# Expert weights in one 16 KB piece per partition, and transposes that read columns with a step

## The chip, the cores and the metric

The kernel runs on one core of one Trainium2 chip. The metric is device time in microseconds (us), from one launch of the whole kernel; lower is better. TensorE's granted clock has two levels, 2.4 GHz (shown as 1.00) and 1.2 GHz (0.50).

## The reference

One layer of a hybrid decoder on 4096 tokens of width 1024, in float32. The first half (norm, one combined projection, sliding-window attention beside a short gated convolution, output projection) gives `h`. The second half is a mixture of experts: each token goes to the best 1 of 4 groups and there to the best 2 of 8 experts, so there are 8192 assignments over 32 experts.

```python
order = jnp.argsort(eid)                       # assignments sorted by expert
xbuf = zeros.at[dest].set(xt[tok_s])           # blocks of 128 rows, one expert each
def expert_block(args):
    xb, e = args                               # xb: 128 x 1024
    return (jax.nn.silu(xb @ w_g[e]) * (xb @ w_u[e])) @ w_d[e]
y = ybuf[dest] * gate_s[:, None]               # w_g, w_u: 1024 x 512; w_d: 512 x 1024
return jax.ops.segment_sum(y, tok_s, num_segments=n_tok)
```

A sum over the 1024 (or 512) rows of a weight matrix may be taken in any order, as long as the row of the weights and the column of `xb` (or of the activation) that meet are the same.

## The kernel before

It has two parts, one after the other. `mixer` walks over 32 tiles of 128 tokens and writes `h` to the output, the normed rows to `hn_rows` in HBM, and for each expert a list of its tokens and gates, `slot_table`. `experts` then walks over 32 experts and, for each, over its blocks of 128 assignments (at least one; the counts come from the routing, 80 blocks in all here).

A block goes like this. GpSimd reads the block's slots (token number and gate, L1286), gathers 128 rows of `hn_rows` into `xg` by an indirect DMA (L1254), and scatters an earlier block's `y` into the output with an add (L1266). TensorE turns `xg` (128 tokens x 1024) with 8 transposes of 128 x 128 (`transpose_rows`, L1338), ScalarE and VectorE copy the result out of PSUM as two fp32r parts `gT_hi` and `gT_lo`. Then come 24 matmuls for gate (psA) and 24 for up (psB): 8 chunks of 128 rows of the weights, each as hi x hi, lo-weight x hi and hi-weight x lo. The product with silu, `act_rows` (128 x 512), is turned with 4 transposes (`turn_act`, L1345), and 24 matmuls with down fill psF and psG. TensorE issues in the order gate(b), turn_act(b), up(b), transpose_rows(b + 1), down(b), where turn_act and down work on the block before. In a transpose the rows to be turned are the stationary operand (the weight load) and the identity matrix is the moving one.

The weights of an expert are three matrices of 2 MB. They lie raw in `raw["gate"]`, `raw["up"]` and `raw["down"]`, each 128 partitions x 8 x 512 float32 in the space of `wi_all`. SP issues the three loads of the next expert (`load_expert`, L168) as soon as ScalarE and VectorE have split the raw weights of the present one into `hi` and `lo` (L1424, L1466), which they do once for each expert. There is one raw buffer and one split buffer for each matrix. The loads of expert 0 are issued earlier, in the mixer's last full tile (L389), on the same SP queue as the mixer's own DMAs: behind them stand one load of `xres`, the four transposing DMAs of the probabilities, and what follows.

Chunk k of a matmul takes `raw[...][:, k, :]`, on partition p. Before, for gate and up this is row 128 k + p of the matrix, so a partition reads 8 rows of 2 KB that lie 256 KB apart. For down, whose rows are 4 KB, a partition reads 4 rows that lie 512 KB apart; index k of the 8 is then row chunk k // 2 and column half k % 2, and the matmuls use it in that way (L1355). Accordingly transpose c of `xg` takes its columns 128 c to 128 c + 127, which are adjacent in SBUF.

Of the kernel before, what the change touches and what calls it, by code (L numbers as in the profile page):

```python
# [34 lines left out]
P = 128  # L35
D = 1024
KD = D // P
# [11 lines left out]
KE = DE // P  # L49
# [89 lines left out]
def build(nc, x, meta_tokens, rel_bias, mix_norm_g, w_in, q_norm_g, k_norm_g, attn_sinks, conv_w,  # L139
          attn_out_norm_g, conv_out_norm_g, w_out, ffn_norm_g, w_group_router, b_group_router,  # L140
          w_expert_router, b_expert_router, w_gate, w_up, w_down, consts, onehot, out):
    x2 = x.rearrange("b s d -> (b s) d")
    table = nc.dram_tensor("slot_table", [E * CAP, 2], I32).ap()
    hn_dram = nc.dram_tensor("hn_rows", [SEQ + P, D], F32).ap()
    u_dram = nc.dram_tensor("u_rows", [(TILES + 1) * P, CC], F32).ap()
    band_dram = nc.dram_tensor("band_rows", [P, HEADS * BW], F32).ap()

    def bcast(a, n, offset=0):

        return bass.AP(a.tensor, a.offset + offset, [[0, P], [1, n]])  # L150

    with ExitStack() as keep:
        def ksb(name, shape, dt):
            return keep.enter_context(nc.sbuf_tensor(name, shape, dt))

        cst = ksb("cst", [P, CW], F32)
        ident = cst[:, C_ID:C_ID + P]
        blocks_of = ksb("blocks_of", [P, 2 * E], I32)

        held = keep.enter_context(nc.semaphore("held"))  # L160

        wi_all = ksb("wi_all", [P, KD + 1, 2 * IN], F16)
        wi_flat = wi_all[:].rearrange("p s c -> p (s c)").bitcast(F32)
        raw = {n: wi_flat[:, j * 4096:(j + 1) * 4096].rearrange("p (k n) -> p k n", k=8)
               for j, n in enumerate(("gate", "up", "down"))}
        raw_in = {n: keep.enter_context(nc.semaphore(f"raw_in_{n}")) for n in raw}

        def load_expert(sp, n, e):  # L168

            w = {"gate": w_gate, "up": w_up, "down": w_down}[n]  # L170
            dst = raw[n] if n != "down" else raw[n].rearrange("p (k a) n -> p k (a n)", k=KE)
            sp.dma_start(dst, w[0, bass.ds(e, 1)].rearrange("o (k p) n -> p (o k) n", p=P)).then_inc(raw_in[n], 16)

        psA, psB, psC, psD, psE, psF, psG, psH = (
            keep.enter_context(nc.psum_tensor(f"ps{c}", [P, 512], F32)) for c in "ABCDEFGH")
        with ExitStack() as ctx:
            mixer(nc, ctx, locals())
        with ExitStack() as ctx:
            experts(nc, ctx, locals())
# [1004 lines left out]
def experts(nc, ctx, env):  # L1184
    out, table, hn_dram, cst, ident, blocks_of, held, raw, raw_in, load_expert = (env[n] for n in (
        "out table hn_dram cst ident blocks_of held raw raw_in load_expert").split())
    psA, psB, psC, psD, psE, psF, psG = (env[f"ps{c}"] for c in "ABCDEFG")

    def sb(name, shape, dt=F32):
        return ctx.enter_context(nc.sbuf_tensor(name, shape, dt))  # L1190
# [6 lines left out]
    xg = sb("xg", [P, D])  # L1197
    gT_hi, gT_lo = sb("gT_hi", [P, KD, P], F32R), sb("gT_lo", [P, KD, P], F32R)
    gated, act_rows = sb("gated", [P, DE]), sb("act_rows", [P, DE])
# [15 lines left out]
    def walk(eng, block, before=None):  # L1215


        def loads(e):
            n = eng.value_load(blocks_of[0:1, bass.ds(e, 1)], min_val=1, max_val=TILES)  # L1219
            base = eng.value_load(blocks_of[0:1, bass.ds(e + E, 1)], min_val=0, max_val=3 * TILES)  # L1220
            return n, base

        n, _ = loads(0)
        block(0, 0, 0, True)
        block(0, 1, 1, False)
        with eng.If(n > 2):
            with eng.Fori(2, n) as i:
                block(0, i, i, False)
        with eng.Fori(1, E) as e:
            n, base = loads(e)  # L1230
            block(e, 0, base, True)
            with eng.If(n > 1):
                with eng.Fori(1, n) as i:
                    block(e, i, base + i, False)
        n, base = loads(E - 1)
        return base + n
# [3 lines left out]
    @block.sync  # L1240
    def _(sp):

        with sp.Fori(1, E) as e:
            for n in raw:
                sp.wait_ge(hi_s[n], 8 * e)
                sp.wait_ge(lo_s[n], 8 * e)
                load_expert(sp, n, e)
# [73 lines left out]
    @block.tensor  # L1321
    def _(pe):
        def split_mm(ps, l_k, left, right, r_k, fresh, name=None, e=0):

            for n, k in enumerate(l_k):
                if fresh:
                    pe.wait_ge(hi_s[name], e * 8 + r_k[n] + 1)
                    pe.wait_ge(lo_s[name], e * 8 + r_k[n] + 1)
                for j, (l, r) in enumerate(((left[0], right[0]), (left[0], right[1]), (left[1], right[0]))):
                    m = nc.tensor.matmul(ps[:, :], l[:, k, :], r[:, r_k[n], :], start=(n == 0 and j == 0),  # L1330
                                         stop=(n == len(l_k) - 1 and j == 2))
            return m

        def transpose_rows(b):
            pe.wait_ge(rows_in, 16 * (b + 1))
            for h, ps in enumerate((psC, psD)):
                for c in range(4):
                    m = nc.tensor.transpose(ps[:, c * P:(c + 1) * P], xg[:, (4 * h + c) * P:(4 * h + c + 1) * P], ident)  # L1338
                m.then_inc(xgT_ps, 1)

        def turn_act(b):

            pe.wait_ge(act_s, b)
            for c in range(KE):
                m = nc.tensor.transpose(psE[:, c * P:(c + 1) * P], act_rows[:, c * P:(c + 1) * P], ident)  # L1345
            m.then_inc(aT_ps, 1)

        def down(b):

            pe.wait_ge(aT_hi_s, b)  # L1350
            pe.wait_ge(aT_lo_s, b)
            pe.wait_ge(y_act, b + 2)
            pe.wait_ge(y_dve, b + 2)
            for half, ps in enumerate((psF, psG)):
                split_mm(ps, range(KE), (aT_hi, aT_lo), (hi["down"], lo["down"]), [2 * k + half for k in range(KE)],  # L1355
                         False).then_inc(y_ps, 1)

        def block_(e, i, b, first):
            static0 = isinstance(b, int) and b == 0
            pe.wait_ge(xgT_hi, 2 * (b + 1))  # L1360
            pe.wait_ge(xgT_lo, 2 * (b + 1))
            if not static0:
                pe.wait_ge(silu_s, b)
            split_mm(psA, range(KD), (gT_hi, gT_lo), (hi["gate"], lo["gate"]), list(range(KD)), first, "gate", e
                     ).then_inc(gate_ps, 1)
            if not static0:
                turn_act(b)
            split_mm(psB, range(KD), (gT_hi, gT_lo), (hi["up"], lo["up"]), list(range(KD)), first, "up", e
                     ).then_inc(up_ps, 1)
            transpose_rows(b + 1)  # L1370
            if not static0:

                loaded = 8 * e if first else 8 * (e + 1)
                pe.wait_ge(hi_s["down"], loaded)
                pe.wait_ge(lo_s["down"], loaded)
                down(b)


        pe.sem_inc(y_ps, 4)
        transpose_rows(0)  # L1380
        total = walk(pe, block_)
        turn_act(total)
        pe.wait_ge(hi_s["down"], 8 * E)
        pe.wait_ge(lo_s["down"], 8 * E)
        down(total)
# [137 lines left out]
```

## Time and profile before

| what | value |
|---|---|
| median of 3 runs | 2779.41 us (2779.2 to 2781.75) |
| profiled execution | 2781.87 us, its span 2780.2 us |
| mean granted clock | 0.981 |
| TensorE matmul busy | 2646.1 us (95%) |
| TensorE weight load busy | 1821.8 us (66%) |
| VectorE, ScalarE, GpSimd busy | 62%, 50%, 30% |
| DMA, mean over the span | 178 GB/s |
| weight loads, 32 each of 2048 KB, median to landing | gate 9.4 us, up 12.6 us, down 11.1 us |
| gather into xg, 80 of them, median to landing | 4.5 us |

The span is the time from the first to the last instruction. Busy time of TensorE overlaps with itself, since matmuls are pipelined; what counts is the distance between starts. The mixer ends and the expert stage begins at about 1343 us; the first transposes of the expert stage start at 1353 us.

### The profile page before, as it was taken

How to read it: one execution, taken by the hardware profiler on the slowest of the kernel's cores; microseconds unless marked ns; L12 is line 12 of the kernel's file. 1: busy time of each engine (PE TensorE's matmuls, PEld its weight loads, DVE VectorE, ACT ScalarE, POOL GpSimd, SP SyncE). 2: the span in 40 equal slices, each digit the busy share in tenths (PEclk: the TensorE clock that was granted, in tenths of full speed). 3: DMA queues.
4: the chain of work that ended last, by engine and by line, in shares of the span. 5: the costliest groups of instructions: out<-in, count | busy, mean ns of one | idle time of the engine just before them, and what ended most of it. 6: DMA issues, size and time to landing. Idle time of an engine off the chain costs nothing.

```text
span 2780.2 us, 49854 instructions
## 1 busy us (share of the span) xinstructions
PE 2646.1 (95%) x14252; PEld 1821.8 (66%) x14253; DVE 1720.6 (62%) x3920; ACT 1393.3 (50%) x3046; POOL 831.1 (30%) x825
## 2 busy tenths in 40 slices
PE   4999999999999999994599999999999999999997
PEld 1455555555555555552488888888878888888886
DVE  5677777777777777775445455546545543546543
ACT  7665555556565555652234455445535443445533
POOL 1133333223333332331123333323333322322332
PEclk9899999999999999997799999999999999999999
DMA  8376666666666666666456677676767666567762
GB/s 313 85 160 163 163 155 163 158 149 158 162 166 153 159 159 152 155 155 182 131 155 189 198 227 235 192 221 203 235 189 233 194 189 161 173 186 238 239 182 53
DMA packets 546539, 495.75 MB, mean 178 GB/s; under 512 B 411803, under 2 KB 411964, under 8 KB 545484
## 3 DMA queue, kind: packets, MB, share of 16 engines
q1 hardware_dynamic: 517660, 406.61, 51.7%
q0 software_dynamic: 28848, 88.77, 13.6%
q8 instruction: 14, 0.23, 0.0%
q14 instruction: 17, 0.14, 0.0%
HBM read 310.27 MB, written 87.88 MB: 143 GB/s over the span
## 4 chain that ended last, share of the span: by engine, by line
PE 49%; DMA 2%; issue 0%; DVE 0%; POOL 0%; POOLq 0%; ACT 0%; DVEq 0%; ACTq 0%
PE psB L1330 15%; PE psA L1330 15%; PE psF L1330 8%; PE psG L1330 7%; PE psC L1338 1%; PE psD L1338 1%; PE psE L1345 1%; DMA xg<-hn_rows,slots 1%; DMA slots<-slot_table 1%; DMA out_rows<-y,rows_of_y 0%; DVE down_lo L1466 0%; DVE y L1473 0%; POOL out_rows L1266 0%; ACT gT_hi L1450 0%; POOLq L1219 0%
## 5 line engine op out<-in xcount | busy, mean ns | idle before, releaser
L476 PE MATMUL psG<-wi_all,both_xT 128*128 128x512 f16 x1536 | 346.1, 382 | 11.2 <-DMA both_xT<-x 11.2
L476 PEld LDWEIGHTS psG<-wi_all,both_xT 128*128 128x128 f16 x1536 | 148.9, 98 | 189.0 <-DMA both_xT<-x 11.4
L1254 POOL DMA_INDIRECT xg<-hn_rows,slots x80 | 99.1, 1239 | 538.1 <-DMA slots<-slot_table 400.9
L1330 PE MATMUL psB<-up_hi,gT_hi 128*128 128x512 f32 x632 | 254.3, 402 | 0.0
L1330 PE MATMUL psA<-gate_hi,gT_hi 128*128 128x512 f32 x632 | 246.9, 391 | 3.1 <-ACT gT_hi L1450 1.7
L1466 DVE TENSOR_TENSOR down_lo<-wi_all,down_hi 128x512 fp32r<-128x512 f32 x256 | 157.0, 685 | 147.4 <-ACT down_hi L1424 147.4
L1330 PE MATMUL psB<-up_hi,gT_lo 128*128 128x512 f32 x632 | 247.5, 392 | 0.0
L1330 PE MATMUL psA<-gate_hi,gT_lo 128*128 128x512 f32 x632 | 246.8, 390 | 0.0
L1330 PE MATMUL psA<-gate_lo,gT_hi 128*128 128x512 f32 x632 | 246.6, 390 | 0.0
L1330 PE MATMUL psB<-up_lo,gT_hi 128*128 128x512 f32 x632 | 246.3, 390 | 0.0
L1450 ACT ACTIVATE gT_hi<-psC 128x512 fp32r<-128x512 f32 x80 | 47.8, 597 | 386.4 <-PE psC L1338 386.4
L1480 DVE TENSOR_TENSOR act_rows<-psB,gated 128x512 f32<-128x512 f32 x79 | 54.6, 691 | 291.1 <-PE psB L1330 291.1
L1424 ACT ACTIVATE down_hi<-wi_all 128x512 fp32r<-128x512 f32 x256 | 137.0, 619 | 149.5 <-PE psG L1330 149.5
L1263 POOL COPY rows_of_y<-slots 128x1 int32<-128x1 int32 x80 | 129.3, 1616 | 244.0 <-DVE y L1473 243.1
L667 ACT ACTIVATE prob<-prob,soft,s_stat 128x256 f32<-128x256 f32 x256 | 150.6, 589 | 80.0 <-DVE soft L985 79.8
L1466 DVE TENSOR_TENSOR gate_lo<-wi_all,gate_hi 128x512 fp32r<-128x512 f32 x256 | 157.0, 685 | 46.7 <-ACT gate_hi L1424 46.7
L476 PE MATMUL psC<-wi_all,both_xT 128*128 128x512 f16 x792 | 178.1, 380 | 4.9 <-DVE wi_all L952 4.9
L476 PE MATMUL psD<-wi_all,both_xT 128*128 128x512 f16 x792 | 177.8, 380 | 0.0
L476 PE MATMUL psE<-wo_all,both_mT 128*128 128x512 f16 x768 | 172.7, 382 | 1.8 <-DMA both_mT<-prob 1.8
L476 PE MATMUL psF<-wo_all,both_mT 128*128 128x512 f16 x768 | 171.0, 379 | 0.0
L1466 DVE TENSOR_TENSOR up_lo<-wi_all,up_hi 128x512 fp32r<-128x512 f32 x256 | 156.6, 681 | 0.9 <-ACT up_hi L1424 0.9
L808 POOL TENSOR_TENSOR yc<-u,w_cv 128x512 f32<-128x512 f32 x32 | 40.6, 1269 | 389.9 <-DMA um<-u_rows 389.9
(302 smaller groups left out, 5907.7 us busy)
## 6 DMA issues: line engine op xcount, KB each, us to landing
wi_all<-in_w_gate SPq DMA_DIRECT2D x32, 2048.0 KB, 9.4
wi_all<-in_w_up SPq DMA_DIRECT2D x32, 2048.0 KB, 12.6
wi_all<-in_w_down SPq DMA_DIRECT2D x32, 2048.0 KB, 11.1
xt<-in_x SPq DMA_DIRECT2D x32, 512.0 KB, 3.7
um<-u_rows SPq DMA_DIRECT2D x64, 256.0 KB, 2.8
xres<-in_x SPq DMA_DIRECT2D x32, 512.0 KB, 4.6
out_rows<-h SPq DMA_DIRECT2D x32, 512.0 KB, 3.2
hn_rows<-xres SPq DMA_DIRECT2D x32, 512.0 KB, 2.9
```

The source lines that it names most:

```text
L476: m = nc.tensor.matmul(ps, left[:, l, k, :], weights.half(r, k, n, width), start=(k == 0 and j == 0), stop=(k == KD - 1 and j == 2))
L667: s.activation(prob[:, hd, :], prob[:, hd, :], ACT.Exp, bias=ntop[:, hd:hd + 1], scale=inv_s, accum_out=psum_[:, hd:hd + 1]).then_inc(p_sb ...
L808: g.tensor_tensor(yc[:], u[:], w_cv[:, 2, :], ALU.mult).then_inc(cv.sem, 1)
L1254: pool.indirect_dma_start(xg[:], None, hn_dram, bass.IndirectOffsetOnAxis(ap=slots[:, 0, 0:1], axis=0), bounds_check=SEQ + P - 1).then_inc ...
L1263: g.tensor_copy(rows_of_y[:], slots[:, 3, 0:1]).then_inc(named, 1)
L1330: m = nc.tensor.matmul(ps[:, :], l[:, k, :], r[:, r_k[n], :], start=(n == 0 and j == 0), stop=(n == len(l_k) - 1 and j == 2))
L1338: m = nc.tensor.transpose(ps[:, c * P:(c + 1) * P], xg[:, (4 * h + c) * P:(4 * h + c + 1) * P], ident)
L1345: m = nc.tensor.transpose(psE[:, c * P:(c + 1) * P], act_rows[:, c * P:(c + 1) * P], ident)
L1424: s.activation(hi[n][:, k, :], raw[n][:, k, :], ACT.Copy).then_inc(hi_s[n], 1)
L1450: s.activation(gT_hi[:, 4 * h:4 * h + 4, :].rearrange("p k c -> p (k c)"), ps[:, :], ACT.Copy).then_inc(xgT_hi, 1)
L1466: v.tensor_tensor(lo[n][:, k, :], raw[n][:, k, :], hi[n][:, k, :].bitcast(F32), ALU.subtract).then_inc(lo_s[n], 1)
L1480: v.tensor_tensor(act_rows[:], psB[:, :], gated[:], ALU.mult).then_inc(act_s, 1)
```

## The change

A partition now reads one piece of 16 KB: rows 8 p to 8 p + 7 of gate and up, or rows 4 p to 4 p + 3 of down. Chunk k of a matmul then holds row 8 p + k (or 4 p + k) on partition p. So that the same rows and columns meet, transpose number k of `xg` takes columns k, 8 + k, 16 + k, ... (128 columns with a step of 8 floats), and transpose c of `act_rows` takes columns c, 4 + c, 8 + c, ... (a step of 4 floats). The number of instructions, of DMAs and of bytes stays the same, as do all waits.

```diff
         def load_expert(sp, n, e):
 
             w = {"gate": w_gate, "up": w_up, "down": w_down}[n]
-            dst = raw[n] if n != "down" else raw[n].rearrange("p (k a) n -> p k (a n)", k=KE)
-            sp.dma_start(dst, w[0, bass.ds(e, 1)].rearrange("o (k p) n -> p (o k) n", p=P)).then_inc(raw_in[n], 16)
+            sp.dma_start(raw[n].rearrange("p k n -> p (k n)"),
+                         w[0, bass.ds(e, 1)].rearrange("o (p k) n -> p (o k n)", p=P)).then_inc(raw_in[n], 16)
...
             for h, ps in enumerate((psC, psD)):
                 for c in range(4):
-                    m = nc.tensor.transpose(ps[:, c * P:(c + 1) * P], xg[:, (4 * h + c) * P:(4 * h + c + 1) * P], ident)
+                    m = nc.tensor.transpose(ps[:, c * P:(c + 1) * P], xg[:].rearrange("t (p k) -> t k p", k=KD)[:, 4 * h + c, :], ident)
                 m.then_inc(xgT_ps, 1)
...
             for c in range(KE):
-                m = nc.tensor.transpose(psE[:, c * P:(c + 1) * P], act_rows[:, c * P:(c + 1) * P], ident)
+                m = nc.tensor.transpose(psE[:, c * P:(c + 1) * P], act_rows[:].rearrange("t (p k) -> t k p", k=KE)[:, c, :], ident)
             m.then_inc(aT_ps, 1)
```

## Rows read from the trace of the kernel before

**Rows 1.** Chain of waits, expert stage (start us, length us, what).

```profile
1963.09 5.50 PE psB L1330 x24
2038.63 5.49 PE psB L1330 x24
...
2091.79 5.49 PE psB L1330 x24
2109.51 5.50 PE psB L1330 x24
```

**Rows 2.** Waits of the weight loads, 1390 to 2760 us (total us, times, longest us).

```profile
PEld psC L1338 <- DMA xg<-hn_rows,slots: 4.1, 5, 3.3
```

**Rows 3.** Timeline of SP's queue and of TensorE in the mixer's tail.

```profile
1257.95 4.75 SPq L172 DMA_DIRECT2D wi_all<-in_w_down  x1
1265.36 15.82 SPq L375 DMA_TRANSPOSE wi_all<-prob  x4
...
1280.69 1.44 PE L574 MATMUL psA<-V,wi_all 128*128 128x128 f16 x16 [11.72 <-DMA wi_all<-prob]
1284.80 1.46 PE L574 MATMUL psB<-V,wi_all 128*128 128x128 f16 x16 [2.68 <-DMA wi_all<-prob]
```

**Rows 4.** Windows: length, busy PE, PEld, DVE, ACT, POOL, clock, DMA share, GB/s.

```profile
15.00:25.00 10.00, 1.75 (x3) 0.33 (x1) 2.31 (x3) 7.80 (x8) 0.00 (x0) 1.00 1.01 427
1262.00:1269.00 7.00, 6.96 (x33) 2.94 (x30) 5.86 (x11) 4.63 (x13) 6.08 (x4) 1.00 1.04 391
1270.50:1275.50 5.00, 0.00 (x0) 0.00 (x0) 0.42 (x4) 0.12 (x1) 2.02 (x2) 0.60 1.03 407
```

**Rows 5.** Gathers, loads, transposes: timeline of GpSimd, SP and PEld, and the chain.

```profile
1551.61 1.23 POOL L1254 DMA_INDIRECT xg<-hn_rows,slots  x1 [8.36 <-DMA slots<-slot_table]
1552.12 0.37 SPq L172 DMA_DIRECT2D wi_all<-in_w_gate  x1
...
1977.99 1.17 POOL L1254 DMA_INDIRECT xg<-hn_rows,slots  x1 [5.63 <-DMA slots<-slot_table]
1985.91 0.14 PEld L1338 LDWEIGHTS psC<-cst,xg 128*128 128x128 f32 x1
...
2014.84 9.69 DMA xg<-hn_rows,slots
2016.21 0.37 SPq L172 DMA_DIRECT2D wi_all<-in_w_down  x1
2024.57 0.42 PEld L1338 LDWEIGHTS psC<-cst,xg 128*128 128x128 f32 x4 [3.26 <-DMA xg<-hn_rows,slots]
...
2123.24 1.44 POOL L1254 DMA_INDIRECT xg<-hn_rows,slots  x1 [8.14 <-DMA slots<-slot_table]
2123.97 0.37 SPq L172 DMA_DIRECT2D wi_all<-in_w_gate  x1
...
DMA to landing us min/median/max: 4.2/4.5/9.8
```

**Rows 6.** Timeline of TensorE (PE matmul, PEld weight load) around one block's transposes.

```profile
1968.42 0.60 PE L1338 MATMUL psC<-cst,xg 128*128 128x128 f32 x4
1968.86 0.60 PE L1338 MATMUL psD<-cst,xg 128*128 128x128 f32 x4
...
1968.75 0.47 PEld L1338 LDWEIGHTS psD<-cst,xg 128*128 128x128 f32 x4
1969.18 0.19 PEld L1330 LDWEIGHTS psF<-down_hi,aT_hi 128*128 128x128 f32 x1
1969.29 0.19 PEld L1330 LDWEIGHTS psF<-down_lo,aT_hi 128*128 128x128 f32 x1
```

**Rows 7.** Groups by shape (busy us, mean ns, idle), then line L1338 (min/median/max ns).

```profile
L476 PEld LDWEIGHTS psG<-wi_all,both_xT 128*128 128x128 f16 x1536 | 148.9, 98 | 189.0 <-DMA both_xT<-x 11.4 <-issue 6.1
L1330 PEld LDWEIGHTS psF<-down_hi,aT_hi 128*128 128x128 f32 x316 | 60.0, 190 | 12.1 <-issue 2.0
...
L1338 PEld LDWEIGHTS psC<-cst,xg x320: 138/140/232, 1353.2 to 2753.0; 128*128 128x128 f32 x160
```

## The prediction

> **What bounds the kernel now.** I read the granted clock and the span first (one core, 0.981 over 2780.2 us), then the page's chain of waits, then the waits of TensorE, then the same windows on the DMA side, and last the timeline around every gather of the expert stage. The page's slices split the span in two: the mixer (up to slice 18), and from 1353 us on the expert stage, where all that the change touches lies, except the first expert's three loads, which are issued at 1257 us.
>
> In the expert stage the chain runs along TensorE. One block takes 17.72 us, from one psB group of 24 matmuls to the next [rows 1]. In 1390 to 2760 us the weight loads of TensorE wait for only one thing, the gather, and for 4.1 us in total, 3.3 of them in one place [rows 2]. Around it, four blocks take 75.54 us (1963.09 to 2038.63) where 4 x 17.72 = 70.88 would do: 4.66 us over, about 3.1 of waiting and 1.6 in which TensorE is granted 1.2 GHz after it stood idle. So what is saved on transfers inside this stage can bring about 5.5 us at most (4.66, and 0.8 of shorter waits), while each nanosecond added to a TensorE instruction is paid in full.
>
> **The change, part by part.** It has two halves. The loads of gate and up go from eight 2 KB pieces for each partition to one of 16 KB, and those of down from four of 4 KB to one of 16 KB. The price is that the 8 transposes of the gathered rows and the 4 of the activation read their columns with a step: 32 bytes and 16 bytes between elements instead of 4.
>
> *Expert 0's load, in the mixer's tail.* The three loads go out on SP's queue at 1257 us, ahead of one row load and the four transposing DMAs of the probabilities; the four take SP 15.82 us to issue, and TensorE waits 11.72 us for them with nothing else to do [rows 3]. So a microsecond off these loads is a microsecond off the span. Rates from rows: pieces of 2 KB move at 391 GB/s, of 4 KB at 407, and the w_in load (9 KB pieces) at 427 [rows 4]. I take 427 for 16 KB, the nearest and longest there is. Two loads of 2.097 MB: 2 x (5.36 - 4.91) = 0.90 us; the third 5.15 - 4.91 = 0.24 us. Saving 1.1 us. Bounds: 0 (pieces are cut into the same packets) and 14.4 us (11.72 and the second wait of 2.68, if the transposes no longer stood behind the loads at all, which one queue makes unlikely).
>
> *The other 31 experts' loads.* They cost nothing now. A load lands 9.4 to 12.6 us after its issue by the page's medians, and the same buffer is issued again no sooner than 35.4 us later (two blocks); its reader comes some 30 us after the issue. TensorE's work is the cover, and it is gone only at about three times the landing time. Value 0.
>
> *The gathers.* The typical one is issued at 1977.99, lands 4.5 us later, and its transposes start at 1985.91, so 3 us or more are spare; seven of the 80 collide with a weight load that is issued 0.5 to 1.4 us behind them and land 8.6 to 9.8 us after their issue, just when TensorE wants them (the first and the last of the seven, and the one that holds TensorE up by 3.26 us, in [rows 5]). The gather then ends about 8.3 us after that load's issue (2014.84 + 9.69 against 2016.21; the others of the seven within 0.2 us of it), so it ends with the load that it collides with. A gate load that takes 0.45 us less brings it in 0.45 us sooner. That removes the four short waits (0.8 us) and, with two late gathers in a row before the long one, 0.9 to 1.1 of its 3.1 us. Value -1.9 us. Bounds: -5.5 us (the gather slips out ahead of the load and the low clock goes too) and +29 us (second rival). What would be late next on this path is the y copy of VectorE behind the split of down, which the change does not touch.
>
> *The stepped transposes.* Identity is the moving operand and the rows are the weights, so the step falls on the weight load. Now four transposes take 0.44 us, 110 ns each, and a weight load starts together with the matmul before it [rows 6]. A weight load of the fp32r matmuls lasts 190 ns instead of 141 [rows 7], and the one at 1969.18, which stands behind a transpose, still lets the next start 0.11 us later [rows 6]. So 49 ns more fit under a 110 ns transpose. How much of the 141 ns is the reading of the columns: 42 ns more than for fp16 (98), at most the 92 ns by which the load grows at 1.2 GHz (140 to 232, [rows 7]); 128 columns at one per cycle of 2.4 GHz give 53, which lies between. If a stepped read takes twice that, 106 ns, it still fits. No row shows a stepped weight read, so the bounds are wide: below, 0 (a read cannot be faster than the contiguous one it replaces, and it is hidden); above, one 16-byte line for each element where a line gives four now, 4 x 53 = 213 ns, so 103 ns more for each of the 640 + 316 transposes, 99 us. I take 2 ns each, since the nearest row is the fp32r load that fits: 956 x 2 ns = +1.9 us.
>
> The Trainium skill speaks against this half: "Advanced Engine Details and Errata", section SBUF Cachelines, says that SBUF is read in lines of 16 bytes, that at least two hits on a line are needed to hide the access, and that another line at each access is penalised. Here each element is on its own line in both kinds of transpose. It gives no size; read as half rate it changes nothing in the sum above, read as a full line each it is the first rival. No row of this case decides it.
>
> **Sum.** -1.1 - 1.9 + 1.9 = -1.1 us. The profiled execution took 2781.87 us around its span of 2780.2; it becomes 2780.8. It lies 2.46 us over the median of the runs (2779.41), so the forecast for the median is 2778.3 us. A difference under 0.2% (5.6 us) cannot be told from no change here.
>
> **Rivals.** *First, slower: the stepped weight load becomes the bound.* Place: the 12 transposes of each block; it decides from a weight load of more than 110 ns of reading, against 53 now. At three times, 160 ns, 956 x 50 ns = 48 us, 2826 us. At four times, 99 us, 2877 us. For it: each element is its own line, and nothing hides TensorE in this stage. Against it: half the window is free. It is one mechanism with two prices.
>
> *Second, slower: long pieces hold the queue.* A 16 KB piece occupies an engine 16384 x 16 / 427 GB/s = 0.61 us, and a gather has 8 rows for each engine. If the row packets have to wait behind single long pieces of the gate load and then of the up load as well, I put the seven colliding gathers 2.5 us later: 17.5 us, and 7 x 1.6 us at 1.2 GHz behind the stalls, 29 us in all: 2807 us. Against it: a load has only 8 such pieces for each engine, 4.9 us in all, so even behind all of them the gather ends no later than it does now. The Trainium skill has it that an engine goes round its queues by packets ("DMA: Bandwidth & Descriptors", section Queues, rings and completion order); the collisions in the trace fit a gather that shares with the load.
>
> *Third, faster beyond noise.* The load ends early enough for the late gathers to come free: -5.5 us here, -1.1 in the tail, and nothing for the transposes: 2772.8 us, and lower if the tail gives more than its rates say. For it: the collisions are decided by a microsecond. Against it: the shift that I can show is half of one.
>
> *Fourth, it does not do what it says.* The pieces are cut into the same packets: no gain, transposes +1.9 us, 2781.3 us, within the noise.
>
> **How the numbers follow.** Forecast 0.50, fourth 0.07: within 0.2% 0.57. Third 0.13: faster. First 0.24 (0.10 around three times, 0.14 at four times) and second 0.06: slower 0.30. The likeliest case alone is 2773 to 2784. The range goes from 2771 up to 2832: it takes in the second rival and the partial form of the first, and leaves out the fourfold price (0.14) and a little below, 0.17 in all.
>
> **What will show it.** In the timeline, four transposes again in 0.44 us and a psB-to-psB distance of 17.72 us: the read is hidden; any growth times 80 blocks is the whole result. A weight load of the transposes above 141 ns with the matmul distance unchanged means that the line rule holds and costs nothing. In the DMA rows, the rate of 1262 to 1269 us should rise to about 427 GB/s, the pieces be 16 KB, and the wait of 11.72 us be near 10.6. The gather's longest landing should be 9.3 rather than 9.8 us, and TensorE's wait for it under 4.1 us. I am wrong if the block distance changes at all, or if a gather that had 3 us to spare becomes late.

## The result

The change makes the kernel slower: 2788.56 us median over 17 runs (2783.25 to 2799.32) against 2779.2 us over 17 runs of the kernel before beside them (2777.11 to 2784.43). The ratio is 1.0039, 95% interval 1.003 to 1.0048, some 11 us. The forecast was 2778.3 us, 1.1 us less than before. The runs after are spread over 16 us, those before over 7; that spread turned out to be part of the answer.

The profiled execution after has a span of 2790.3 us against 2780.2, at the same mean clock (0.981). The instructions are the same in number on every engine. What the loads' hardware queue moved (packets, MB, share of 16 engines), before and then after:

```profile
q1 hardware_dynamic: 517660, 406.61, 51.7%
q1 hardware_dynamic: 448028, 406.61, 50.1%
```

That is 69632 packets fewer, exactly what one packet for each piece gives (64 loads of gate and up with 896 pieces fewer each, 32 of down with 384), so a 16 KB piece is one packet. Where the 10.1 us lie can be read from five places of the two traces.

The first are the chain of waits after, at the start of the expert stage, in its middle and at its end (start us, length us, what):

```profile
1361.49 10.42 DMA xg<-hn_rows,slots
1371.96 0.73 PE psC L1338 x4
1374.79 7.22 PE psA L1330 x24
1382.48 5.48 PE psB L1330 x24
...
2081.86 5.48 PE psB L1330 x24
2099.62 5.48 PE psB L1330 x24
...
2757.62 5.48 PE psB L1330 x24
```

The block distance is 17.76 us instead of 17.72 [rows 1]: 0.04 us a block, and a change of the whole stage.

Second, the weight loads of the transposes, by shape (busy us, mean ns, then idle), which answer to [rows 7]:

```profile
L1345 PEld LDWEIGHTS psE<-cst,act_rows 128*128 128x128 f32 x316 | 50.4, 204 | 5.7
L1338 PEld LDWEIGHTS psC<-cst,xg 128*128 128x128 f32 x320 | 47.8, 191 | 38.2 <-DMA xg<-hn_rows,slots 32.2
L1338 PEld LDWEIGHTS psD<-cst,xg 128*128 128x128 f32 x320 | 42.4, 193 | 0.0
```

They took 139 to 143 ns before. With a step of 8 floats a load takes some 50 ns more, with a step of 4 floats 65 ns more.

Third, what the weight loads waited for from 1358 us on (before: 4.1 us, 5 times, as in [rows 2]), and what GpSimd waited for before it could issue a gather, 1375 to 2760 us (before: 388.7 us in total, 8.5 at most):

```profile
PEld psC L1338 <- DMA xg<-hn_rows,slots: 9.3, 6, 4.3
...
POOL xg L1254 <- DMA slots<-slot_table: 416.0, 56, 11.7
```

GpSimd now waits up to 11.7 us for the slot load, 1 KB, and TensorE's waits for gathers have more than doubled in sum. One of them is new and stands at the very start: the gather of 1361.49 takes 10.42 us; the same gather before, issued at 1360.89 us, landed after 5.70 us and did not hold TensorE up. The load of up was issued 1.21 us behind it after, 1.64 us before.

Fourth, a collision of a gather with a load (timeline of GpSimd, SP and PEld, then the chain), which answers to [rows 5]:

```profile
2022.13 1.42 POOL L1254 DMA_INDIRECT xg<-hn_rows,slots  x1 [10.43 <-issue]
2022.75 0.33 SPq L171 DMA_DIRECT2D wi_all<-in_w_down  x1
2032.19 0.52 PEld L1338 LDWEIGHTS psC<-cst,xg 128*128 128x128 f32 x4 [4.32 <-DMA xg<-hn_rows,slots]
...
2022.13 10.01 DMA xg<-hn_rows,slots
...
DMA to landing us min/median/max: 4.2/4.6/10.4
```

From the issue of the load to TensorE's start are 9.44 us (2032.19 - 2022.75). In the kernel before they were 8.36, for the same load of down. The same for a gate load (chain and SP's timeline), before and then after:

```profile
1993.94 9.80 DMA xg<-hn_rows,slots
1995.27 0.37 SPq L172 DMA_DIRECT2D wi_all<-in_w_gate  x1
...
1964.61 10.12 DMA xg<-hn_rows,slots
1965.73 0.33 SPq L171 DMA_DIRECT2D wi_all<-in_w_gate  x1
```

The gather landed 8.47 us after the load's issue before, 9.00 us after. All eight late gathers of the trace before landed 8.0 to 8.5 us after the issue of the load that they met, all six of the trace after 8.9 to 9.4 us.

Fifth, the mixer's tail: windows (columns as in [rows 4]) and the timeline of TensorE and SP, which answer to [rows 3, 4]:

```profile
1262.00:1269.00 7.00, 7.00 (x34) 3.22 (x33) 5.92 (x12) 5.10 (x13) 6.76 (x5) 1.00 1.00 418
...
1258.07 0.33 SPq L171 DMA_DIRECT2D wi_all<-in_w_gate  x1
1281.45 1.44 PE L574 MATMUL psA<-V,wi_all 128*128 128x128 f16 x16 [11.32 <-DMA wi_all<-prob]
1283.05 1.46 PE L574 MATMUL psB<-V,wi_all 128*128 128x128 f16 x16 [0.16 <-DMA wi_all<-prob]
```

The loads do move faster, 418 GB/s instead of 391. In the same window of the other executions, 2 KB pieces of gate and up as whole loads moved at 358 to 391 GB/s and 16 KB pieces at 398 to 437.

The account, in us of the two profiled executions:

| part | before | after | difference |
|---|---|---|---|
| up to the issue of expert 0's gate load | 1256.90 | 1258.07 | +1.2 |
| from there to the first transpose of the expert stage | 96.3 | 95.3 | -1.0 |
| from there to psB of the second block | 25.0 | 29.1 | +4.1 |
| from there to psB of the last block | 1369.2 | 1375.1 | +5.9 |

The first line is the mixer itself, which the change does not touch: over the profiled executions of this study the stage's first transpose, without the one kernel whose loads were slow, came anywhere from 1351.6 to 1358.5 us, so 1 us in it means nothing. Nor does 1.0 us in the second line: steps_only, whose loads are those of before, has 94.4 us there. Of the last line, 77 x 0.04 = 3.1 us are the longer blocks, and the other 2.8 are waits for gathers and the low clock behind the long one. So the stage pays some 3.1 us for the steps and 6.9 us for late gathers, in this execution.

### The profile page after: what moved, and what is told of

The parts are those of the page before. It is cut to its first block, busy times and chain, and to the rows that moved or that the text cites. A ratio compares the mean times of both kernels' runs of the same rounds, so it can differ in the third digit from the quotient of the medians.

```text
span 2790.3 us, 49854 instructions
## 1 busy us (share of the span) xinstructions
PE 2652.4 (95%) x14252; PEld 1836.1 (66%) x14253; DVE 1720.4 (62%) x3920; ACT 1393.4 (50%) x3046; POOL 820.9 (29%) x825
## 4 chain that ended last, share of the span: by engine, by line
PE 42%; DMA 6%; issue 2%; POOL 1%; DVE 1%; POOLq 0%; ACT 0%; ACTq 0%; DVEq 0%
PE psB L1330 13%; PE psA L1330 13%; PE psF L1330 7%; PE psG L1330 6%; DMA xg<-hn_rows,slots 3%; DMA slots<-slot_table 3%; PE psC L1338 1%; PE psE L1345 1%; PE psD L1338 1%; POOL rows_of_y L1263 1%; DVE gate_lo L1466 0%; DMA out_rows<-y,rows_of_y 0%; DVE y L1473 0%; DVE down_lo L1466 0%; POOL out_rows L1266 0%
## 5 line engine op out<-in xcount | busy, mean ns | idle before, releaser
L1263 POOL COPY rows_of_y<-slots 128x1 int32<-128x1 int32 x80 | 116.7, 1459 | 233.2 <-DVE y L1473 232.6
```

Of the source, the lines that this page charges most:

```text
L1263: g.tensor_copy(rows_of_y[:], slots[:, 3, 0:1]).then_inc(named, 1)
```

## The experiments

The first four kernels of the table shared a chip and runs of the kernel before, and so did the next four and the last four. A ratio is to those runs, with its 95% interval. In steps_only, pieces_only, paced_16k and step_map the columns turned and the rows of the weights do not match, so they serve for the time only. First the table, then each one.

| kernel | pieces gate, up / down | steps rows / activation | median us (runs) | ratio, interval |
|---|---|---|---|---|
| steps_only | 2 / 4 KB | 8 / 4 | 2781.73 (11) | 1.0011 (1.0002 to 1.002) |
| pieces_only | 16 / 16 | 1 / 1 | 2783.99 (11) | 1.0012 (1.0001 to 1.0024) |
| gateup_4k | 4 / 4 | 2 / 1 | 2783.83 (11) | 1.0019 (1.001 to 1.0028) |
| gateup_8k | 8 / 4 | 4 / 1 | 2790.94 (5) | 1.0037 (1.0023 to 1.0051) |
| gateup_16k | 16 / 4 | 8 / 1 | 2784.97 (12) | 1.0021 (1.001 to 1.0033) |
| down_16k | 2 / 16 | 1 / 4 | 2779.98 (12) | 1.0002 (0.9991 to 1.0012) |
| paced_2k | 2 / 4, halves | 1 / 1 | 2781.65 (12) | 1.0002 (0.9992 to 1.0012) |
| paced_16k | 16 / 16, halves | 1 / 1 | 3031.72 (6) | 1.0849 (1.08 to 1.0898) |
| before_paced | 2 / 4, halves | 1 / 1 | 2777.5 (11) | 0.9994 (0.9985 to 1.0003) |
| after_paced | 8 / 8, halves | 8 / 4 | 2780.93 (11) | 1.0003 (0.9994 to 1.0012) |
| after_again | 16 / 16 | 8 / 4 | 2792.44 (10) | 1.0039 (1.0026 to 1.0051) |
| step_map | 2 / 4 | 3 and 6 / 2 | 2795.86 (1) | one run, no interval |

### Steps alone

```diff
-  transpose(ps[...], xg[:, (4 * h + c) * P:(4 * h + c + 1) * P], ident)
+  transpose(ps[...], xg[:].rearrange("t (p k) -> t k p", k=KD)[:, 4 * h + c, :], ident)
-  transpose(psE[...], act_rows[:, c * P:(c + 1) * P], ident)
+  transpose(psE[...], act_rows[:].rearrange("t (p k) -> t k p", k=KE)[:, c, :], ident)
```

> The stepped transposes alone, with the loads of before (rows and columns of the weights no longer match, so this kernel leaves the reference's sum and is for time only). Theory A (the long pieces hold the DMA queue and put GpSimd's chain late; the steps cost only what the block distance shows): four activation transposes in 0.47 us instead of 0.44, block distance 17.76 instead of 17.72 us, so +3 to +4 us over before, about 2783, and TensorE's wait for gathers after 1390 us as before (about 4 us). Theory B (the steps cause the loss, the late gathers are a consequence of the changed block distance): +7 to +11 us, with a new or longer wait for a gather.

Measured: 1.0011, about 3 us. Two neighbouring blocks in its chain of waits, and what its weight loads waited for from 1358 us on:

```profile
2090.53 5.48 PE psB L1330 x24
2108.29 5.48 PE psB L1330 x24
...
PEld psC L1338 <- DMA xg<-hn_rows,slots: 1.1, 3, 0.6
```

17.76 us between blocks, as after, and less waiting than before, 1.1 us in all, where theory B asked for more. Theory A's half on the steps holds.

### Pieces alone

```diff
-  sp.dma_start(dst, w[0, bass.ds(e, 1)].rearrange("o (k p) n -> p (o k) n", p=P))
+  sp.dma_start(raw[n].rearrange("p k n -> p (k n)"),
+               w[0, bass.ds(e, 1)].rearrange("o (p k) n -> p (o k n)", p=P))
```

> The 16 KB pieces alone, transposes as before (rows and columns of the weights no longer match, for time only). Theory A: block distance back at 17.72 us, but slots that land up to 12 us after their issue, a second gather of 10 us around 1361 to 1371 us, and more waiting of TensorE for gathers: +4 to +8 us over before, with a wide spread between runs in steps of some 4 to 5 us. Theory B: no slower than before, within 2 us of it.

Measured: 1.0012, the eleven runs from 2778.5 to 2796.84 us. The chain (the first three rows) and the waits of its profiled execution, which at 2796.84 us is the longest of the eleven:

```profile
1362.74 10.26 DMA xg<-hn_rows,slots
1383.57 5.50 PE psB L1330 x24
1401.29 5.49 PE psB L1330 x24
...
PEld psC L1338 <- DMA xg<-hn_rows,slots: 15.4, 10, 4.3
```

The block distance is back at 17.72 and the late gathers are there, ten of them, the one at the start among them. Theory B is out: pieces alone bring the late gathers, without any step. The lower end of the interval is near 1, so the time by itself would be weak evidence; the trace carries it. The ten late gathers landed 8.8 to 9.4 us after the issue of the load that they met, as in the kernel after.

### Pieces of 4 and of 8 KB for gate and up

```diff
+  dst = raw[n].rearrange("p (a j) n -> p a (j n)", j=J)              # J = 2 or 4
+  src = w[0, bass.ds(e, 1)].rearrange("o (a p j) n -> p (o a) (j n)", p=P, j=J)
...
+  xg[:].rearrange("t (a p j) -> t a j p", p=P, j=J)[:, (4 * h + c) // J, (4 * h + c) % J, :]
```

> Gate and up in four pieces of 4 KB for each partition, their transposes with a step of 2 floats (two elements on each 16-byte line); down and its transposes as before. Theory A, with the piece length as the cause: a piece holds an engine for 0.16 us, as one of down does now, so the gathers stay as they are, the step is hidden (weight load between 141 and 165 ns, distance 17.72 us), and the tail gains 0.5 us: 2776 to 2781, not to be told from before. Theory C (any step of more than one float costs the same as a step of 8): weight load 190 ns, time still that of before.

> Gate and up in two pieces of 8 KB, their transposes with a step of 4 floats; down as before. Theory A: a piece holds an engine for 0.31 us, half of the 16 KB one, so slots and gathers are late by about half as much: 0 to +5 us over before. If a step of 4 floats is what makes a weight load last 204 ns instead of 192 (in the kernel after the change the activation has this step and the rows have 8), then the eight row transposes now take 0.47 us for each four, and the distance becomes 17.72 + 8 x 0.011 = 17.80 us, +6 us more; if the 204 ns come from where the activation's transposes stand, the distance stays at 17.72 us.

For gateup_4k the expectation on the step was wrong. Its line L1343 (min/median/max ns of the weight load), the chain, and the landing of gathers:

```profile
L1343 PEld LDWEIGHTS psD<-cst,xg x320: 208/209/226, 1352.6 to 2753.9; 128*128 128x128 f32 x160
...
2089.31 5.48 PE psB L1335 x24
2107.11 5.48 PE psB L1335 x24
...
DMA to landing us min/median/max: 4.2/4.5/9.2
```

A step of 2 floats makes the weight load 204 to 209 ns long, more than a step of 8 does, and the block 17.80 us long: 78 x 0.08 = 6.2 us, which is all of its 1.0019. Its longest landing is 9.2 us, below the 9.8 of the kernel before, and TensorE never waits for a gather after the first block. Its six late gathers landed 7.7 to 7.9 us after the gate load's issue, sooner than the 8.0 to 8.5 of the kernel before. So 4 KB pieces of gate and up are harmless to the gathers.

For gateup_8k the weight loads take 206 and 214 ns and the blocks are 17.82 us apart (2060.31 to 2095.94 is two), close to the 17.80 that the expectation gave for a dear step of 4. That is 78 x 0.1 = 8 us of its 1.0037 (10 us). In its profiled execution, the longest of its five, 8 gathers are waited for, 12.7 us in all, with a longest landing of 10.4 us, and those that met a gate load landed 9.0 to 9.2 us after its issue. The slope is not with the length of the piece in proportion, as I had put it: for a gather that collides, 8 KB is already as bad as 16.

### Gate and up, or down

```diff
# gateup_16k: the new load for gate and up, the new transposes of xg; down and act_rows as before
# down_16k:   the new load for down, the new transposes of act_rows; gate, up and xg as before
```

> Gate and up in one 16 KB piece with row transposes of step 8; down and the activation's transposes as before. Steps: the block distance keeps only the row transposes' share, 17.735 us (0.015 above before, so +1.2 us over the stage). Pieces, theory A1 (two 16 KB loads back to back, gate and up, are what holds GpSimd's packets): late gathers as in the kernel after the change, a first one at 1362 to 1372 us, in all 2783 to 2788. Theory A2 (down's 16 KB load does it, since the scatter and the slot load stand behind it): no more stalls than before, 2779 to 2782.

> The other half: down in 16 KB pieces and the activation's transposes with step 4; gate, up and the row transposes as before. Steps: block distance 17.745 us (0.025 above before, +2 us over the stage), since the activation's weight load of 204 ns does not fit under its matmul of 110 ns. Theory A1: no new stall, the second gather lands in 5 us, 2780 to 2783. Theory A2: late gathers as in the kernel after the change, 2784 to 2789.

Waits of the weight loads from 1358 us on, gateup_16k first, then down_16k with two blocks of its chain:

```profile
PEld psC L1343 <- DMA xg<-hn_rows,slots: 7.5, 9, 1.1
```

```profile
PEld psC L1343 <- DMA xg<-hn_rows,slots: 2.4, 3, 2.0
...
2090.36 5.48 PE psB L1335 x24
2108.09 5.48 PE psB L1335 x24
```

Gate and up carry most of the loss (1.0021), down next to none (1.0002); the intervals just touch. That fits theory A1, but not the reason in it, two loads back to back: in the ten traces with whole loads 64 of 75 late gathers met a gate load, so gate alone may carry it, whatever follows. Part of the 1.0021 is steps: 78 x 0.03 = 2.3 of 5.8 us. The four gathers that met a 16 KB load of down, with nothing behind it, landed 9.3 to 9.5 us after its issue, later than any that met gate.

A1 failed in one more detail. The late gather at the very start came in down_16k and not in gateup_16k. What tips it is the distance of the two issues. The load of up was issued 1.16 to 1.43 us behind this gather in the four executions that have it late (down_16k, after, pieces_only, after_again), and 1.47 us or more behind it in the other six with whole loads. The whole stage says the same: in the ten traces with whole loads, a load came less than 1.5 us behind a gather 77 times, and 74 of these gathers took more than 8 us to land; it came 1.5 to 4 us behind 359 times, and one of these gathers did.

Blocks in down_16k are 17.73 us apart and in gateup_16k 17.75 us, so the row transposes, at step 8, account for 0.03 of the 0.04 us, and those of the activation, at step 4, for 0.01.

### Loads in two halves

```diff
             half = (KD if n != "down" else KE) // 2
+            sp.dma_start(dst[:, 0:half], src[:, 0:half]).then_inc(raw_in[n], 16)
+            sp.wait_ge(raw_in[n], landed)              # the first half has landed
+            sp.dma_start(dst[:, half:], src[:, half:]).then_inc(raw_in[n], 16)
```

> The kernel before, with each of the loads of experts 1 to 31 issued in two halves of 1 MB, the second only when the first has landed (pieces still 2 KB, or 4 KB for down). If a load's descriptors in the queue are what GpSimd's packets wait behind, a gather that collides waits for 2.6 us of load at most instead of 5.4, the longest landing falls from 9.8 us to 7 or less, and the stall of 3 us with its low clock is gone in every run: 2775.5 to 2778, less spread than before. If the landing time is set by something else (VectorE's splits that slow GpSimd's descriptor writing), the longest landing stays over 9 us and the time at 2779.

> The 16 KB pieces of pieces_only (contiguous transposes, for time only: rows and columns of the weights do not match), each load issued as two halves of 64 partitions, the second when the first has landed. If the queue's backlog is what turns long pieces into late gathers, this brings pieces_only back to before or below: 2776 to 2780 and no second gather of 10 us. If the length of one piece does it by itself, the stalls stay: 2781 to 2787, as in pieces_only.

paced_2k was inconclusive in its time, 2781.65 us where 2775.5 to 2778 was expected. Its profiled execution waits for one gather, 1.9 us, instead of five, and its latest row packet comes 8.5 us after the gather's issue, where a landing within 7 was expected. But expert 0's loads were cut as well and TensorE got its first probabilities at 1282.40 us instead of 1280.69.

paced_16k was a badly made experiment. Its halves were partitions 0 to 63 and 64 to 127, and these move at little more than half the rate. The window of 1262 to 1269 us and the waits from 1358 us on:

```profile
1262.00:1269.00 7.00, 7.00 (x37) 3.32 (x36) 6.41 (x20) 6.40 (x18) 6.44 (x5) 1.00 1.05 225
...
PEld psC L1342 <- DMA xg<-hn_rows,slots: 201.7, 29, 22.8
```

225 GB/s with the DMA engines shown busy. It says nothing on the question, but it shows what loads that take longer do to gathers. So I cut along the rows of a partition instead and left expert 0's loads whole:

> The kernel before, with the loads of experts 1 to 31 in two halves, the second issued when the first has landed; expert 0's loads stay whole, so the mixer's tail is that of before (in paced_2k they were cut too, and TensorE got its probabilities 1.7 us later). If the backlog of a load in the queue is what gathers wait behind, the expert stage has no stall of 3 us with its low clock: from the first to the last psB group 78 blocks of 17.72 us and less than 1 us over (before: 4.7 over, the first block apart), and 2775 to 2778. If it is something else, 2779 as before.

> The kernel after the change with the loads of experts 1 to 31 in two halves (each partition's 16 KB piece cut into two of 8 KB), the second when the first has landed. If the loss is backlog behind long pieces, what is left is the steps: before plus 3 us, less up to 1 us of the tail, 2779 to 2783, against about 2788 for the kernel after the change on the same chip, with the collisions landing in 7 us or less. If the length of a piece costs by itself, 2785 or more.

> The kernel after the change once more, beside the two others on one chip. If steps (about +3) and pieces (about +3.5) add up, its time is some 6.5 us over before, about 2786; if they make each other worse, it stays at 9 to 11 over, about 2789.

after_paced first (the chain, and waits from 1358 us on), then the same waits of before_paced, then of after_again:

```profile
2088.85 5.48 PE psB L1336 x24
2106.61 5.48 PE psB L1336 x24
...
PEld psC L1344 <- DMA xg<-hn_rows,slots: 1.4, 1, 1.4
```

```profile
PEld psC L1345 <- DMA xg<-hn_rows,slots: 2.3, 1, 2.3
```

```profile
PEld psC L1338 <- DMA xg<-hn_rows,slots: 11.6, 9, 4.4
```

On one chip the kernel after takes 2792.44 us, and with each load cut in two 2780.93: 11.5 us come back, with the same steps (17.76 us a block) and the same order of rows. The eleven runs lie within 4.1 us, where the kernel after has 15. What a step costs is still there, since before_paced is 3.4 us faster than after_paced. Cutting also halves the piece to 8 KB, but gateup_8k shows that 8 KB pieces with the whole load in the queue are no better. So 8 KB pieces, which go with late gathers when a whole load is in the queue, do not hurt here.

The traces show two effects of the cut, and the 11.5 us do not part them. A gather that meets half a load ends sooner: in before_paced the last row packet of such a gather came 6.0 to 6.7 us after the load's issue (8 gathers), in the kernel before 7.5 to 8.0; in after_paced it was 5.8 us for the only one, in after_again 8.4 to 8.8 for nine. That fits a backlog: bytes of a load that stand in the queue when GpSimd's gather comes. And the cut moves the issues: in after_paced only one gather had a load less than 1.5 us behind it, in after_again nine, and at the start of the stage the load of up came 2.4 us behind the gather instead of 1.4. How much of the gain is shorter collisions and how much is fewer of them, no run shows.

before_paced is the best version of the study, 2777.5 us, but its interval (0.9985 to 1.0003) holds no change, so it is not shown to beat the kernel before. It still has one wait of 2.3 us, and from the first to the last psB group 2.1 us more than 78 blocks of 17.72, where less than 1 was expected.

after_again lies 12 us (by medians) over the kernel before (ratio 1.0039 again), and the sum of the two halves alone is 1.0023. By the medians they make each other worse; by the intervals (the sum may reach 1.0044) that is not shown.

### Other steps

```diff
-  xg[:, (4 * h + c) * P:(4 * h + c + 1) * P]       # psC, psD
+  xg[:, 0:(3, 6)[h] * P].rearrange("t (p j) -> t j p", j=(3, 6)[h])[:, c % 3, :]
-  act_rows[:, c * P:(c + 1) * P]                   # psE
+  act_rows[:].rearrange("t (a p j) -> t a j p", p=P, j=2)[:, c // 2, c % 2, :]
```

> The kernel before with other steps in its transposes (time and weight load only; the columns turned are not the right ones): the first four row transposes (psC) step 3 floats, the last four (psD) step 6, the activation's (psE) step 2. By the 16-byte line rule steps under 4 floats should cost less than steps above (psC and psE at most 165 ns, psD 190). By what the runs so far showed (step 1: 141 ns, step 8: 191, steps 2 and 4: 202 to 214) the short steps are no cheaper than the long ones: psE 200 or more, psC 200, psD between 190 and 215.

```profile
L1338 PEld LDWEIGHTS psD<-cst,xg 128*128 128x128 f32 x320 | 50.0, 233 | 0.0
L1345 PEld LDWEIGHTS psE<-cst,act_rows 128*128 128x128 f32 x316 | 49.8, 202 | 6.1
L1338 PEld LDWEIGHTS psC<-cst,xg 128*128 128x128 f32 x320 | 49.1, 196 | 35.7 <-DMA xg<-hn_rows,slots 29.5
```

Step 2: 202 ns, step 3: 196, step 6: 233, and from the other kernels step 4: 204 to 214, step 8: 191 to 193, no step: 139 to 145. The short steps are no cheaper, as the second reading had it; that step 6 would go over 215 it did not foresee. The block distance is 17.87 us, 78 x 0.15 = 12 us for the stage, and it waited 29 us for its first gather (23 before); the two make up most of what its one run, 2795.86 us, lies over the kernel before.

## Why the prediction was wrong

**What held.** TensorE's chain bounds the stage, and the gather is the only thing that it waits for. The other experts' loads still cost nothing by themselves. Pieces are packets, so the fourth rival is out. The doubled price of a stepped read was nearly hidden, so the fourfold price of the first rival (99 us) was far off.

**The tail: right in direction, its size not shown.** The forecast was 1.1 us and a wait of 10.6 us for the probabilities. The wait fell from 11.72 to 11.32 us, and TensorE had its first probabilities 23.4 us after the issue of expert 0's gate load instead of 23.8. Over the executions this takes 22.9 to 23.8 us with 2 KB pieces and whole loads (before, steps_only, before_paced, step_map) and 22.0 to 23.4 us with 16 KB pieces for gate and up (after, after_again, after_paced, pieces_only, gateup_16k). The means differ by 0.9 us, about what was forecast, but the ranges overlap.

**The steps: right mechanism, small term.** I put 2 ns on each of 956 transposes, 1.9 us. Measured is 0.04 us a block, 3.1 us over the 78 distances between 79 blocks (the 80th gather has no matmuls, so the 80 blocks named before the prediction are one too many). A weight load of 192 ns in the rows costs 4 ns for each transpose, one of 204 ns in the activation 3 ns. What each would cost could not be read from the trace before: the nearest row, the fp32r load of 190 ns, was right for the length of a load at step 8, but it does not fit under 110 ns at no cost.

**The gathers: the step that failed.** The prediction said that a gate load that takes 0.45 us less brings the colliding gather in 0.45 us sooner, -1.9 us. It comes later instead, 8.9 to 9.4 us after the load's issue where there were 8.0 to 8.5, and the late gathers cost 6.9 us more than before in the profiled execution. I had read that a colliding gather ends with the load, and took the load's end as its cause. The trace before did not say so: the gate loads that met a gather landed 10.2 to 10.7 us after their issue, 2 us behind the gather. After, they landed at 8.2 to 8.4 us, ahead of it. So at a collision long pieces let the load gain 2 us and the gather lose 0.6. (Eight gathers are late in the trace before, not seven, and they end 8.0 to 8.5 us after the load's issue, not within 0.2 us of 8.3.)

How pieces do that can be followed in part, since the traces hold the single DMA packets, a gather's 128 rows and the pieces of the gate load that it meets:

| pieces of gate | first row packet after the load's issue, us | all rows move in, us | load's pieces meanwhile, for each row | gather lands after the load's issue, us |
|---|---|---|---|---|
| 2 KB (before) | 4.1 to 4.4 | 3.2 to 3.9 | 2.4 to 3.7 | 8.0 to 8.5 |
| 4 KB (gateup_4k) | 4.3 to 4.5 | 2.7 to 3.0 | 1.2 to 1.4 | 7.7 to 7.9 |
| 8 KB (gateup_8k) | 4.5 to 5.0 | 3.5 to 4.1 | 1.0 to 1.2 | 9.0 to 9.2 |
| 16 KB (after) | 4.4 to 4.7 | 3.8 to 4.2 | 0.5 to 0.6 | 8.9 to 9.0 |

A 16 KB piece takes its engine 0.61 us and a gather has 8 rows for each engine; one piece for each row would make 4.9 us, and that is not what happens. Most of the delay of a collision comes before the first row moves: a gather that meets nothing starts its rows some 2 us after its own issue, one that meets a load more than 4 us after the issue of that load. What makes it stand that long is open, and so is why 4 KB is better than 2. The slot load's longest wait went from 8.5 to 11.7 us, and so GpSimd issues the next gather later; in which way the slot load is held up was not followed.

Both signs of being wrong that the prediction named came true: the block distance changed (17.72 to 17.76 us), and a gather with 3 us to spare, the second of the stage, became late. The longest landing was to be 9.3 us and is 10.4; the waits were to be under 4.1 us and are 9.3.

**The second rival was the right one, with the wrong argument against it.** It gave "long pieces hold the queue" a chance of 0.06 and 29 us. I argued that even behind all of a load's pieces the gather ends no later than it does now. It does end later, behind nearly all of the gate load: 1.1 to 1.3 MB of its 2.1 move before the first row and 1.1 to 1.3 MB more until the last, part of them up's; before it was 0.8 and 0.6 to 1.0 MB. The argument also leaves out that one late GpSimd DMA delays those behind it. The chain after shows such a series (start us, length us), which ends in the longest stall:

```profile
1936.30 11.05 DMA slots<-slot_table
...
1956.23 7.40 DMA slots<-slot_table
1964.61 10.12 DMA xg<-hn_rows,slots
...
2011.10 8.66 DMA slots<-slot_table
2022.13 10.01 DMA xg<-hn_rows,slots
```

Its price, 29 us, was too high because a colliding gather comes some 0.6 us later and not 2.5, and because most stalls are 0.3 to 1 us and leave the clock up. Those of 3 us and more, none to two in an execution, cost 3 to 6 us each, and the one at the start, a wait of 2.5 us with 3.4 us of low clock behind it, 4.1.

**The chances.** I counted all that a faster transfer could save (5.5 us) and called each nanosecond on TensorE expensive, and yet weighed the change near zero. Gathers without slack, decided by a microsecond, should have counted for more on the slow side: there the time is not smooth, and every delay of a gather is paid at once.

## What to carry to other kernels

Pieces of 8 or 16 KB raise a load's own rate (391 to 418 GB/s here for 16) and make a gather that meets the load 0.6 us later, while 4 KB did not; where small transfers feed the engine that bounds the kernel and the bulk load has slack, cut the bulk load and let the first part land before the second is issued, or keep the load's issue more than 1.5 us behind the small transfer's (the second is read from the traces and was not tried by itself). Before accepting a layout for the sake of the loads, list how many small DMAs arrive with no time to spare: if some do, runs spread out and the median moves by whole stalls. A step in the operand that TensorE loads as weights costs 50 to 90 ns for each float32 load of 128 columns. Most of it hides beside the matmuls, but not all: at least 3 ns for each transpose were left in every kernel here.

## What the runs showed of the hardware that I had not expected

- The Trainium skill ("Advanced Engine Details and Errata", section SBUF Cachelines) has it that hits on one 16-byte line run at full speed and other lines are penalised. For TensorE's float32 weight loads the measurement differs: a step of 2 floats, two elements on each line, costs more (202 to 209 ns) than a step of 8 floats with a line for each element (191 to 193). The dearest was step 6 (233).
- Of transposes that stand 110 ns apart, stepped weight loads of 192 ns add 4 ns to each (gateup_16k), of 204 ns in the activation 3 ns (down_16k), of 204 and 209 ns in the rows 10 ns (gateup_4k): hidden almost to their end.
- In the window of 1262 to 1269 us loads of 64 partitions move at 225 GB/s, those of 128 partitions at 358 to 437, with the DMA engines shown busy in both.
- A gather lands late when a 2 MB load is issued less than 1.5 us behind it (74 of 77 times), and hardly ever when the load comes 1.5 to 4 us behind (once in 359).
- Behind a wait of 3.3 us for a gather the granted clock stood at 1.2 GHz for 3.4 us (before, from 2025.8 us), and the wait cost 4.7 us; waits of 3.9 to 4.4 us cost 5.1 to 5.8. The same wait of 3.3 us in gateup_8k left the clock at 2.4 GHz and cost 3.2 us, and one of 1.1 us cost 0.9.
